# Weight splits placed earlier or later around the two scans, and the first merge product ahead of the last gates

## The reference

```python
p = jnp.einsum('bsd,dn->bsn', h, w_in[l])            # h = rmsnorm(x)
(qa, ka, va, qkv_g, z, a_f, a_b, b_f, b_b, gate_a, gate_g) = jnp.split(p, split_at, axis=-1)
oa = diff_attention(...)                              # first attention
ya = jnp.einsum('bse,ed->bsd', oa.reshape(b, s, DA_V), w_proj_attn[l])
qkv_g = jax.nn.silu(centred_depthwise_conv(qkv_g, conv_w[l]))
o_fwd = gated_delta_rule_chunked(qg, kg, vg, g_f, beta_f)
o_bwd = flip(gated_delta_rule_chunked(flip(qg), flip(kg), flip(vg), flip(g_b), flip(beta_b)))
og = rmsnorm(o_fwd + o_bwd, gdn_norm_w[l])            # per head of 128
og = og * jax.nn.silu(z.reshape(b, s, GDN_HEADS, GDN_DV))
yg = jnp.einsum('bse,ed->bsd', og.reshape(b, s, GDN_VW), w_proj_gdn[l])
merged = jax.nn.sigmoid(gate_a) * ya + jax.nn.sigmoid(gate_g) * yg
x = x + jnp.einsum('bsd,de->bse', merged, w_out[l])
```

## Time and profile before

| what | us |
|---|---|
| median of three runs | 3076.32 (3074.25 to 3076.85) |
| the profiled execution | 3077.67 |
| its span in the trace | 3075.9 |
| TensorE busy in it | 2673.9 |
| VectorE, ScalarE, GpSimd busy | 915.9, 760.0, 582.6 |
| mean granted TensorE clock | 0.927 of full |

### The profile page before, as it was taken

The page is one execution under the profiler, slowest core; times in us unless marked ns, Lnnn a source line. Parts: engine busy times, 40 slices in busy tenths (PEclk is TensorE's granted clock), DMA queues, the critical chain, the costliest instruction groups (busy, mean ns, idle before and its releaser), DMA issues.

```text
span 3075.9 us, 33752 instructions
## 1 busy us (share of the span) xinstructions
PE 2673.9 (87%) x14207; PEld 1750.6 (57%) x14207; DVE 915.9 (30%) x1606; ACT 760.0 (25%) x1290; POOL 582.6 (19%) x173
## 2 busy tenths in 40 slices
PE   7989878877999798988988988888968889889998
PEld 5756766666566533323323323365747756678886
DVE  2357654662111311011011011024473421241121
ACT  3247633622011100100100100144241121332222
POOL 3310452532112000000000000021300012234442
PEclk9999979879999899999999999998975689999999
DMA  4301212203223499999999999841100032322222
GB/s 138 110 28 35 92 40 96 69 2 123 68 83 113 171 426 427 428 429 428 429 429 428 429 428 427 365 154 52 62 0 8 1 109 96 117 63 104 91 96 78
DMA packets 130850, 559.33 MB, mean 182 GB/s; under 512 B 7256, under 2 KB 88480, under 8 KB 103080
## 3 DMA queue, kind: packets, MB, share of 16 engines
q1 hardware_dynamic: 129864, 551.28, 45.1%
q0 software_dynamic: 864, 6.29, 0.5%
HBM read 547.01 MB, written 10.54 MB: 181 GB/s over the span
## 4 chain that ended last, share of the span: by engine, by line
PE 70%; DMA 13%; DVE 10%; ACT 5%; issue 3%; POOL 1%; DVEq 0%; SPq 0%; ACTq 0%; POOLq 0%
DMA S<-in_w_up 11%; PE PS L563 8%; PE PS L565 8%; PE PS L564 8%; PE PS L2043 7%; PE PS L2020 6%; PE PS L555 4%; PE PS L2005 2%; PE PS L2992 2%; PE PS L3118 2%; PE PS L3120 2%; PE PS L3121 2%; PE PS L2054 1%; PE PS L2797 1%; PE PS L548 1%
## 5 line engine op out<-in xcount | busy, mean ns | idle before, releaser
L2290 POOL TENSOR_TENSOR r_block<-S,r_block 128x2048 fp32r<-128x2048 f32 x57 | 261.9, 4595 | 1519.8 <-ACT r_block L2279 1511.0
L2020 PE MATMUL PS<-S 128*64 128x512 f32 x2048 | 458.0, 596 | 81.7 <-DMA S<-in_w_up 73.6
L563 PE MATMUL PS<-r_block,r_block 128*128 128x512 f32 x1040 | 418.6, 402 | 10.8 <-DVE r_block L536 4.7
L565 PE MATMUL PS<-r_block,r_block 128*128 128x512 f32 x1040 | 405.8, 390 | 0.0
L564 PE MATMUL PS<-r_block,r_block 128*128 128x512 f32 x1040 | 405.5, 390 | 0.0
L2020 PEld LDWEIGHTS PS<-S 128*64 128x64 f32 x2048 | 140.2, 137 | 391.9 <-issue 244.1
L489 POOL TENSOR_TENSOR r_block<-S,r_block 128x2048 fp32r<-128x2048 f32 x40 | 182.9, 4574 | 496.0 <-ACT r_block L481 487.2
L2043 PE MATMUL PS<-S 128*64 128x512 f32 x1024 | 225.6, 597 | 6.0 <-DMA S<-in_w_down 2.7
L563 PEld LDWEIGHTS PS<-r_block,r_block 128*128 128x128 f32 x1040 | 195.6, 188 | 58.0 <-issue 8.0
L564 PEld LDWEIGHTS PS<-r_block,r_block 128*128 128x128 f32 x1040 | 195.8, 188 | 45.2 <-issue 6.0
L565 PEld LDWEIGHTS PS<-r_block,r_block 128*128 128x128 f32 x1040 | 195.7, 188 | 41.5
(11 more groups left out here) (454 smaller groups left out, 3728.9 us busy)
## 6 DMA issues: line engine op xcount, KB each, us to landing
S<-in_w_gate SPq DMA_DIRECT2D x64, 2048.0 KB, 18.0
S<-in_w_up SPq DMA_DIRECT2D x64, 2048.0 KB, 21.2
S<-in_w_down SPq DMA_DIRECT2D x64, 2048.0 KB, 25.6
S<-in_w_in SPq DMA_DIRECT2D x57, 1024.0 KB, 5.1
S<-in_w_up SPq DMA_DIRECT2D x16, 1024.0 KB, 5.6
S<-in_w_down SPq DMA_DIRECT2D x16, 1024.0 KB, 4.8
S<-decay_rows SPq DMA_DIRECT2D x8, 1024.0 KB, 7.0
S<-in_w_out SPq DMA_DIRECT2D x8, 1024.0 KB, 5.0
```

Of the source, the lines that this page charges most:

```text
L563: pe.matmul(out, wh, r32(HT[:, dc, :]), start=(dc == 0), stop=False)
L565: mm = pe.matmul(out, wl, r32(HT[:, dc, :]), start=False, stop=(dc == DC - 1))
L2020: mm = pe.matmul(PS[c * CAP:(c + 1) * CAP, 2 + 2 * m + g, :], XE[:, 2 * q + r, e * CAP:(e + 1) * CAP], w[:, r, 1024 * g + 512 * c:1024 * g ...
L2290: pool.tensor_tensor(r32(w), w, rounded(WH[k % 2]), ALU.subtract).then_inc(sem("w2_low"), 1)
```

## The change

The whole diff:

```diff
--- before.py
+++ after.py
@@ -1252,7 +1252,7 @@
             for j in range(12 + 2):
                 gi = 12 * gr + j
                 if j < 12:
-                    if j % 2 == 0 and gi:
+                    if j % 2 == 0 and gi not in (0, 12):
                         split_act(act, after(("g", gr, j // 2)))
                     act.wait_ge(*count("gp_proj", gi + 1))
                     act.wait_ge(*count("pads", 1))
@@ -1333,7 +1333,6 @@
 
         def group_pool(pool, gr):
             if gr:
-                split_pool(pool, ("g", gr, 0))
                 split_pool(pool, ("g", gr, 1))
             for j in range(8):
                 n = 8 * gr + j
@@ -1584,8 +1583,7 @@
             act.activation(warm, eps, ACT.Ln).then_inc(sem("zn_ln"), 1)
             for hl in range(HG):
                 act.activation(ZN[gr][:, hl, :], OG[:, HG * gr + hl, :], ACT.Square).then_inc(sem("zn_sq"), 1)
-            if gr:
-                split_act(act, ("z", 1))
+            split_act(act, ("z", 1) if gr else ("g", 1, 1))
             for hl in range(HG):
                 act.wait_ge(*count("zn_sum", HG * gr + hl + 1))
                 act.activation(ZN[gr][:, hl, :], PS[:, 2 + hl, :], ACT.Ln, bias=eps, scale=1.0 / P).then_inc(sem("zn_ln"), 1)
@@ -1620,12 +1618,13 @@
         def gate_act(act):
             head_norms_act(act, 1)
             for h in range(GH):
-                if h % 2 == 0 and h:
-                    split_act(act, after(("z", h // 2)) or ("m", 0, 2))
+                if h in (2, 4):
+                    split_act(act, ("z", h // 2 + 1))
                 act.wait_ge(*count("z_proj", h + 1))
                 if h >= 2:
                     act.wait_ge(*count("z_silu", h - 1))
                 act.activation(ZT[:, h % 2, :], PS[:, Z_BANK[h % 4], :], ACT.Tanh, scale=0.5).then_inc(sem("z_tanh"), 1)
+            split_act(act, ("m", 0, 2))
 
         def gate_dve(dve):
             head_norms_dve(dve, 1)
@@ -1660,6 +1659,8 @@
                     (await_slot if m < 2 else await_split)(pe, ("m", k, m))
                     if k == 0 and m == 0:
                         pe.wait_ge(*count("ot_back", 16))
+                        pe.wait_ge(*count("z_silu", GH - 2))
+                    if k == 0 and m == 1:
                         pe.wait_ge(*count("z_og", GH))
                         pe.wait_ge(*count("z_silu", GH))
                     if k:
@@ -1826,17 +1827,25 @@
                 pool.dma_start(r32(half_at(M_DYN + 16384, s)), htl_dram[:, s * SLOT:(s + 1) * SLOT])\
                     .then_inc(sem("low_back"), 16)
 
+        def first_split_pool(pool, gr):
+
+            for d in range(2):
+                pool.wait_ge(*count(f"sc_r{d}", 3 * (gr + 1)))
+            split_pool(pool, ("z", 0) if gr else ("g", 1, 0))
+
         def GDN_POOL(pool):
             for gr in range(2):
                 if gr:
+                    first_split_pool(pool, 0)
                     low_parts_back(pool, 0)
                 group_pool(pool, gr)
                 heads_pool(pool, gr)
 
 
         def gate_pool(pool):
+            first_split_pool(pool, 1)
             low_parts_back(pool, 1)
-            for j in range(4):
+            for j in range(1, 4):
                 split_pool(pool, ("z", j))
             for k in range(4):
                 for m in (2, 3):
```

## The result

| kernel | median, us | runs |
|---|---|---|
| before | 3076.12 | 3074.25 to 3076.85 |
| after | 3044.97 | 3043.44 to 3046.53 |

The ratio is 0.9903, with a 95% interval of 0.9889 to 0.9917: 31.2 us less. 34.4 were forecast. The span of the profiled execution went from 3075.9 to 3044.7, also 31.2 us.

What follows compares the result with a forecast made beforehand. The prediction took TensorE's stops after the scans and before the merge to bound the kernel. Its terms, 9.8 + 7.6 + 17.0 = 34.4 us, gave 3041.9 us against 3076.32, with a stated range of 3037 to 3052.5.

Steps and rivals of the forecast that it cites:

- The bound: Between first attention and experts the chain is mostly TensorE; its four stops where the change works sum to 30.1 us.
- Scan 0 to group 1: After scan 0, the first transposes of group 1 start at 515.0 instead of 524.8: 9.8 us gained.
- From there at full clock: After scan 0, TensorE goes on from 491.6 at 0.227 us per split matmul; a clock dip would cost 1.7 us.
- the second new wait: In group 1 after scan 0, the transposes wait 1.5 us for the group's first activation.
- so the 3.42 us go completely: In group 1, the second tile's subtraction ends 5.6 us ahead of its use, removing TensorE's 3.42 us stop.
- Scan 1 to the gates: After scan 1, ("z", 1) starts at 721.0 instead of 728.65, with no wait for low parts: 7.6 us gained.
- Gates to merge: The merge starts where the gates end: 13.9 us of wait plus 3.1 us of clock, 17.0 us gained.
- Rival 1: The subtraction holds VectorE in the scans' last chunk, some 7 us together: 3048.9, chance 0.06.
- Rival 2: Low parts after both scans land 3 us later and become the wait, with two clock dips: 3049.9, chance 0.10.
- Rivals 3, 4 and 5: Merge part fails, 3058.9, chance 0.05; gain stops at experts, 3076.3, 0.04; merge clock drops without a stop, 3167, 0.02.
- The sum: The gains at scan 0, scan 1 and merge, 9.8 + 7.6 + 17.0 = 34.4 us, all reach the end.

Runs made afterwards that it cites:

- Part 2: ScalarE's copy of the second tile of group 1, ("g", 1, 1), placed between squares and Ln; alone on the kernel before: 3071.1 us, ratio 0.9981.
- e1: Kernel before with only the first tile's GpSimd subtraction moved into each scan's last chunk: 3057.51 us, ratio 0.9951.
- part 1: The first tile's GpSimd subtraction moved into each scan's last chunk; alone on the kernel before: 3057.51 us, ratio 0.9951.
- e9: Kernel after with the copy of ("g", 1, 1) put back between its head's products: 3042.78 us, ratio 0.9901.
- e2: Kernel before with only the merge's waits changed, first product waiting for six z_silu and second for all: 3058.47 us, ratio 0.9942.
- e3: Kernel before with only the copy of ("m", 0, 2) moved behind the last Tanh: 3062.5 us, ratio 0.9958.
- parts 3 and 4: Copy of ("m", 0, 2) behind the last Tanh, and the merge's smaller first wait; each alone on the kernel before: 3062.5 and 3058.47 us.
- e4: Kernel after with the first tile's subtraction one chunk earlier, beside a VectorE operation with two SBUF inputs: 3046.85 us, ratio 0.9902.
- e6: Kernel after with SyncE starting its next loads only when the low parts have landed: 3041.66 us, ratio 0.9884.
- e8: Kernel after with SyncE's next loads held until the low parts land, and the low parts' first half started once `sc_o0` allows: 3037.15 us, ratio 0.988.

## Why the prediction was right, point by point

- **The bound.** TensorE's stops between the scans and the merge set the time. In the changed kernel the gain made there is there at the end too: the last column is +0.4 us.
- **Scan 0 to group 1: 9.8 forecast, 8.6 measured.** The subtraction, the transfer starts, the high products and the head sums came as worked out. The wait for the low parts was forecast at 2.2 us and was 2.21, the landing at 9.4 to 11.7 and was 9.6 to 11.8. What was mis-sized is "From there at full clock" behind that wait. The low products took 5.53 us and not 3.79: 1.7 us for a dip that I had named, priced right (1.7) and kept for the range. Part of it was covered. The tile's end came closer to the activation's, and the second new wait shrank from the 1.5 us forecast to 0.46.
- **Part 2, "so the 3.42 us go completely".** They go, but not through part 2. Most of them go with part 1, because TensorE waits for the landing anyway (e1: 1.01 left). In the kernel without part 2 that remainder costs nothing in the column (e9: 9.6). I never asked what part 1 alone would leave of them. The sum was right since it priced the two together.
- **Scan 1 to the gates: 7.6 forecast, 7.3 measured,** with the low products at 3.79 us and no wait ahead of them. TensorE stood some 0.9 us between the last L1509 and the first L571.
- **Gates to merge: 17.0 forecast, 17.1 measured.** 13.9 us of wait and the clock of the next 30 us at 1.00 instead of 0.90. e2 and e3 show that parts 3 and 4 cover each other in the same way: 16.6 and 12.9 alone, 17.1 together.
- **Rival 1, VectorE held.** Refuted by L1542 and L1567 at 0.69 us, and by e4 for the right reason. Its price was about right: 4.1 us for a held operation in either scan of e4, where 7 us were put on the two.
- **Rival 2, low parts and clock.** Its time, 3049.9, didn't come, as the landings were not longer. Its mechanism was there in the small: a wait and one dip. e6 and e8 show that this was where the next 3.7 us lay.
- **Rivals 3, 4 and 5.** The merge starts with no wait; the experts' stream, DMA at 0.97 as before, begins 31 us earlier (its first load is issued at 964.5 instead of 995.8); and the 173 us of merge stayed at a clock of 1.00 with no pause ahead of them.
- **The sum.** 34.4 forecast; 8.6 + 7.3 + 17.1 = 33.0 measured at the three places. The other 1.9 us to the 31.1 of the span are the late start (+2.4), a gain of 0.9 in a place that the change doesn't touch, and 0.4 at the end. None of these was forecast; that they stayed small is luck, since the first column alone reaches from -3.3 to +3.8 us in kernels that are the same up to there. The time missed the forecast by 3.1 us, 1.4 of it from my terms.

## What to carry to other kernels

When two edits stand at one place, ask what each leaves for the other: here two parts together brought less than the sum of what each brought alone, in both places (8.6 us against 9.5 and 3.8, 17.1 against 16.6 and 12.9), and one of them (part 2) was worth nothing beside the other. When a compute stall goes, look at the transfer that the stall had hidden, and at what else runs on the DMA engines while it flies; a wait that holds back less urgent loads can be worth more than starting the urgent one earlier. Judge such parts by the distance of two instructions around them, which repeats to some tenths of a microsecond, and not by the whole time, which spreads by several: the two held operations of e4 cost 8.3 us where they stand, and the medians are 1.9 us apart.

## What the runs showed of the hardware

- **A short stop and the clock.** A stop of 2.07 to 2.29 us was followed by some 3.4 us with the clock at 1.2 GHz while TensorE worked (from the rows of 507 to 513 us), in four profiled executions (5.49 to 5.54 us for 16 low products). The clock fell 0 to 0.6 us after TensorE had gone on. After stops of 1.83, 2.15 and 2.07 us the same products took 3.93, 3.94 and 3.92, with the clock at 1.00 in the last. The two last have no part 2, and a second stop of 1.0 us behind them. The length of the stop doesn't tell them apart; what does stays open. Part 2 and the moment of the stop both differ.
- **A held VectorE operation** shows in the trace as a long one: 4.56 us against 0.69, ending 0.6 us after GpSimd's. It made the rest of the scan 4.1 us later, in both scans of e4. Beside the same subtraction, operations with one input in PSUM took 0.68 to 0.69.
- **Two megabytes of transfers started by GpSimd** land in 5.5 to 7.3 us alone, and in 9.0 to 12.2 beside three megabytes started by SyncE.
